# Next expert's down weights issued from ScalarE's queue, in a mixture-of-experts block on one Trainium2 core

## The reference

```python
# 4 groups of 8 experts, each expert 2048 -> 512 -> 2048; top group, then top 2 experts of it
eid = g_sel[:, None] * EXPERTS_PER_GROUP + top_i
gate = g_gate * softmax(top_v)
def expert_block(args):
    xb, e = args
    return (silu(xb @ w_gate[e]) * (xb @ w_up[e])) @ w_down[e]
ys = lax.map(expert_block, (xs, blk_expert))
out = segment_sum(ys * slot_gate[:, None], slot_tok)      # added to x
```

## Time and profile before

| | |
|---|---|
| median of 3 runs | 1783.31 us (1782.98 to 1784.92) |
| the profiled execution | 1783.29 us |
| its span in the profile | 1781.1 us |
| TensorE busy in the span | 1599.1 us (90%) |
| VectorE, ScalarE, GpSimd busy | 651.0, 345.0, 156.9 us |
| bytes moved by DMA | 484.42 MB, mean 272 GB/s |

### The profile page before, as it was taken

One profiled execution on the slowest core, in us unless ns is written; L12 is line 12 of the kernel. 1 busy time (PEld: TensorE's weight loads), 2 busy tenths in 40 slices (PEclk: granted clock), 3 DMA queues, 4 the chain that ended last, 5 costly groups with the idle time before them and its releaser, 6 DMA issues.

```text
span 1781.1 us, 19395 instructions
## 1 busy us (share of the span) xinstructions
PE 1599.1 (90%) x7339; PEld 909.5 (51%) x7339; DVE 651.0 (37%) x856; ACT 345.0 (19%) x612; POOL 156.9 (9%) x223
## 2 busy tenths in 40 slices
PE   7979999989999989939988988898898899889987
PEld 6567788868888445623343333333333334333333
DVE  1376676562223223351331332232132323323234
ACT  3122243452222133301101100100110010101001
POOL 0183024331000000010000000000000000000000
PEclk9989999999999999859999999999999999999999
DMA  7313321127222321319999999999999999999994
GB/s 285 95 32 87 94 72 48 48 71 243 95 95 98 162 79 64 148 37 408 421 421 421 422 421 422 422 421 422 422 422 422 421 422 422 421 421 420 421 421 192
DMA packets 114905, 484.42 MB, mean 272 GB/s; under 512 B 9410, under 2 KB 47404, under 8 KB 61868
## 3 DMA queue, kind: packets, MB, share of 16 engines
q1 hardware_dynamic: 110864, 470.84, 66.3%
q0 software_dynamic: 3264, 12.88, 1.9%
q10 hardware_dynamic: 732, 0.07, 0.0%
HBM read 484.81 MB, written 8.39 MB: 277 GB/s over the span
## 4 chain that ended last, share of the span: by engine, by line
PE 67%; DMA 21%; DVE 7%; issue 2%; ACT 2%; ACTq 0%; SPq 0%; POOL 0%; DVEq 0%; POOLq 0%
DMA weight_ring<-in_expert_w_up_dram 21%; PE ps L1813 17%; PE ps L1466 11%; PE ps L1571 10%; PE ps L1841 7%; PE ps L1680 3%; PE ps L1790 3%; PE ps L1624 3%; DVE residual L1351 2%; PE ps L1791 2%; PE ps L1426 2%; PE ps L1439 2%; PE ps L1706 1%; PE ps L1500 1%; PE ps L1535 1%
## 5 line engine op out<-in xcount | busy, mean ns | idle before, releaser
L1813 PE MATMUL ps<-weight_ring,transposed_acts 128*64 128x512 f32 x2048 | 469.0, 595 | 67.5 <-DMA weight_ring<-in_expert_w_up_dram 66.6
L1813 PEld LDWEIGHTS ps<-weight_ring,transposed_acts 128*64 128x64 f32 x2048 | 153.2, 137 | 377.3 <-issue 253.4
L1351 DVE TENSOR_TENSOR residual<-ps,residual 128x1024 f32<-128x1024 f32 x128 | 151.0, 1220 | 262.4 <-PE ps L1791 262.1
L1841 PE MATMUL ps<-weight_ring,transposed_acts 128*64 128x512 f32 x1024 | 226.8, 595 | 19.1 <-DVE transposed_acts L1358 19.1
L1369 DVE SCALAR_TENSOR_TENSOR y_low<-ps,proj_buffer,y_high 64x1024 fp32r<-64x1024 f32 x64 | 82.1, 1283 | 211.3 <-ACT y_high L851 210.2
L1841 PEld LDWEIGHTS ps<-weight_ring,transposed_acts 128*64 128x64 f32 x1024 | 71.8, 137 | 155.5 <-issue 152.6
L851 ACT ACTIVATE y_high<-ps,proj_buffer 64x1024 fp32r<-64x1024 f32 x64 | 71.0, 1109 | 306.3 <-PE ps L1841 305.4
L1790 PE MATMUL ps<-y_high,spread 128*128 128x512 f32 x256 | 113.8, 445 | 14.5 <-DVE residual L1351 10.4
L1466 PE MATMUL ps<-mix_high,w_in_high 128*128 128x512 f32 x288 | 117.7, 409 | 9.3 <-DVE w_in_low L960 9.3
L843 ACT ACTIVATE transposed_acts<-ps 128x512 f32<-128x512 f32 x32 | 19.1, 598 | 494.4 <-PE ps L1813 494.4
L1466 PE MATMUL ps<-mix_high,w_in_low 128*128 128x512 f32 x288 | 113.3, 393 | 0.0
(11 more groups left out here) (260 smaller groups left out, 1797.6 us busy)
## 6 DMA issues: line engine op xcount, KB each, us to landing
weight_ring<-in_expert_w_gate_dram SPq DMA_DIRECT2D x128, 1024.0 KB, 24.0
weight_ring<-in_expert_w_up_dram SPq DMA_DIRECT2D x128, 1024.0 KB, 25.9
weight_ring<-in_expert_w_down_dram SPq DMA_DIRECT2D x128, 1024.0 KB, 19.0
weight_ring<-in_w_in_dram SPq DMA_DIRECT2D x18, 1024.0 KB, 5.6
weight_ring<-in_w_out_dram SPq DMA_DIRECT2D x16, 1024.0 KB, 5.1
weight_ring<-in_xkv_w_dram SPq DMA_DIRECT2D x8, 1024.0 KB, 6.2
residual<-in_x_dram SPq DMA_DIRECT2D x8, 1024.0 KB, 19.1
weight_ring<-in_xq_w_dram SPq DMA_DIRECT2D x4, 1024.0 KB, 5.4
```

The costliest lines, as they stand in the source:

```text
L1351: v.tensor_tensor(part, ps[:, bank:bank + 2, :].rearrange("p b n -> p (b n)"), part, ALU.add).then_inc(sum_ready if last else part_added, 1)
L1813: ins = mm(ps[side * SLOTS:(side + 1) * SLOTS, 0, :], xsT[:, k, par * SLOTS:(par + 1) * SLOTS], w[:, kk, :], start=(k == 0), stop=(k == KD ...
L1841: ins = mm(ps[half, 4 + n // 2, :], act_t[:, f * SLOTS:(f + 1) * SLOTS], w[:, n * 512:(n + 1) * 512], start=(f == 0), stop=(f == KF - 1), ...
```

## The change

`load_expert` takes a count. In the loop over experts 1 to 31 SyncE issues 8 chunks, the gate and up ones, and ScalarE issues the four down chunks of the next expert, at the end of `block_act`, behind its two copies of the block's result. Their order on ScalarE comes from its own wait for `used`, which stands before the copies and is met when all four down chunks of the block are used. The last block of the 32 issues nothing, so the loop on ScalarE ends one pair earlier and that pair is written out. The blocks beyond the 32 are loaded by SyncE as before.

```diff
--- before.py
+++ after.py
@@ -431,20 +431,20 @@
                     sp.wait_ge(parts_done, 32)
                 sp.dma_start(slot(s), expert_chunk(0, j)).then_inc(landed[s], 16)
 
-            def load_expert(e, b):
-                for j in range(12):
+            def load_expert(e, b, count):
+                for j in range(count):
                     s = expert_slot(j)
                     sp.wait_ge(used, b * 12 + (UE - 12 + j + 1))
                     sp.dma_start(slot(s), expert_chunk(e, j)).then_inc(landed[s], 16)
 
             with sp.Fori(1, NE) as b:
-                load_expert(b, b)
+                load_expert(b, b, 8)
             sp.wait_ge(table_ready, 1)
             more = sp.value_load(meta[0:1, NOVER:NOVER + 1], min_val=0, max_val=NOVER)
             with sp.If(more > 0):
                 with sp.Fori(0, NOVER) as j:
                     e = sp.value_load(meta[0:1, ds(j, 1)], min_val=0, max_val=NE - 1)
-                    load_expert(e, j + NE)
+                    load_expert(e, j + NE, 12)
             for t in range(NT):
                 sp.wait_ge(sum_ready, 2 * t + 2)
                 sp.dma_start(out[0, t * P:(t + 1) * P, :], X[:, t, :]).then_inc(stored, 16)
@@ -837,7 +837,7 @@
             act.wait_ge(top_done, 1)
             a.activation(rq["et"], rq["dt"], ACT.Exp).then_inc(texp_done, 1)
 
-            def block_act(b, par):
+            def block_act(b, par, loads=False):
 
                 act.wait_ge(used, b * 12 + (UE + 8))
                 a.activation(gu, ps[:, 0, :], ACT.Copy).then_inc(gu_copied, 1)
@@ -850,14 +850,20 @@
                     rows = slice(side * SLOTS, (side + 1) * SLOTS)
                     a.activation(y_hi[par * SLOTS:(par + 1) * SLOTS, side:4:2, :], ps[rows, 4:6, :], ACT.Copy,
                                  scale=gate[rows, ds(b, 1)]).then_inc(y_act, 1)
+                if loads:
+                    for j in range(8, 12):
+                        s = expert_slot(j)
+                        act.dma_start(slot(s), expert_chunk(b + 1, j)).then_inc(landed[s], 16)
 
             act.wait_ge(table_ready, 1)
-            block_act(0, 0)
-            block_act(1, 1)
-            with act.Fori(1, NE // 2) as it:
+            block_act(0, 0, True)
+            block_act(1, 1, True)
+            with act.Fori(1, NE // 2 - 1) as it:
                 b = it * 2
-                block_act(b, 0)
-                block_act(b + 1, 1)
+                block_act(b, 0, True)
+                block_act(b + 1, 1, True)
+            block_act(NE - 2, 0, True)
+            block_act(NE - 1, 1)
             more = act.value_load(meta[0:1, NOVER:NOVER + 1], min_val=0, max_val=NOVER)
             with act.If(more > 0):
                 with act.Fori(NE // 2, NBLK // 2) as it:
```

## The result

The changed kernel takes 1818.99 us (1816.48 to 1820.44, 4 runs), the one before 1784.12 us: ratio 1.0193, 95% interval 1.0176 to 1.0211. It is 34.9 us slower; 8 us slower was forecast. The profiled execution took 1816.48 us, its span is 1814.3.

What follows compares the result with a forecast made beforehand. DMA bytes were taken to bound the expert loop. Order 7.0 us, holes 1, ScalarE 0 and start 0 summed to 8 us on 1783.3: 1791.3 us, likeliest case 1787 to 1796, outer range 1782.5 to 1825.

Steps and rivals of the forecast that it cites:

- The bound: Expert loop: DMA bytes at 421 to 422 GB/s set the pace; TensorE has 6 us a pair in hand.
- ScalarE's cost 0: End of each block: four issues, 2.1 us, fit into ScalarE's idle time, so they add 0 us.
- issue 0.4 us after the end of down: End of each block: ScalarE issues down loads 0.4 us after the last down matmul, bounds 0.3 and 2.4.
- Turns: DMA engines in the loop: the two queues are served equally, one 1 MB chunk of each in turn.
- N = 2.8: Even blocks: 2.8 down chunks land ahead of the last up chunk; bounds 1 to 4.
- Paid once, 7.0 us: Whole loop: down chunks landing early cost 7.0 us once, at the end, not per pair; bounds 2.5 to 10.
- Holes: DMA traffic at the end of even blocks: 0.3 us dry a pair, 0 to 4.5 over 15 pairs, taken as 1.
- U: Even block: the moment its last up chunk has landed; down of that block was put 20.6 us later.
- the wait would gather at the last step: Even blocks' gate/up: expected sign, TensorE's wait gathers at the last one or two steps, 3 us and more.
- Rival 1: DMA traffic runs dry each pair or expert: moderate 1806 to 1821 us, far end 1919; chance 0.26.
- Rival 2: Loop's two queues behave as one, or few down chunks land early: cost 0 to 3.5 us, 1783 to 1787; chance 0.16.
- Rival 3: Loop's DMA: a second queue raises the rate to 426 GB/s, giving 1772 or 1779 us; chance 0.10.

Runs made afterwards that it cites:

- e1: Changed kernel plus 24 filler matmuls on TensorE ahead of the last gate/up step of each even block: 2011.05 us, ratio 1.1274.
- e2: Kernel before the change plus the same 24 filler matmuls per even block, as a control: 2008.15 us, ratio 1.1254.
- e5: Changed kernel plus six filler matmuls ahead of the last gate/up step of each even block: 1795.36 us, ratio 1.0065.
- e11: Changed kernel with ScalarE issuing each down chunk as its slot is freed, plus six filler matmuls in even blocks: 1795.56 us, ratio 1.0058.
- e6: Kernel before the change plus six filler matmuls ahead of the last gate/up step of each even block, as a control: 1786.68 us, ratio 1.0010.
- e7: Changed kernel, but ScalarE issues each down chunk as its slot is freed, ahead of its two copies: 1792.85 us, ratio 1.0069.
- e9: Kernel before the change, one queue, but SP issues the four down chunks only after the block's last down matmul: 1785.23 us, ratio 1.0007.
- e4: Changed kernel, but ScalarE issues only odd experts' down chunks, at the end of even blocks; SP issues the rest: 1787.51 us, ratio 1.0020.
- e10: Kernel before, split in order of use: SP issues gate and down chunks 8, 10, ScalarE up and down chunks 9, 11, as slots are freed: 1784.64 us, ratio 0.9998.

## Why the prediction was wrong, step by step

- *The bound.* Right: e1 and e2 show it from the other side, where TensorE is the bound the change costs 3 us.
- *ScalarE's cost 0, and issue 0.4 us after the end of down.* Right: 0.5 us in the pair above.
- *Turns, and N = 2.8.* The mechanism was right, the size a little high for the pair shown: two down chunks landed ahead of the up chunk that ended the wait at 1246.67, at 1239.8 and 1244.7. The turns were equal there: down chunks landed at 1239.8, 1244.7 and 1249.8, gate and up chunks at 1241.6, 1246.6 and 1251.6. The Trainium skill, page "DMA: Bandwidth & Descriptors", section "Queues, rings and completion order", has each DMA engine go round robin between its queue rows; by these rows, the trace agrees.
- *Paid once, 7.0 us.* About right: 8.7 us in e5 and 8.9 in e11 over their control e6, 8.2 in e7 over the kernel before. In e11 nearly all of it is there by the second pair. In e5 only 3.9 us are; its other 4.6 us, 0.3 a pair, look like the small holes of the prediction (its window has 416 GB/s for 421), but the single holes were not measured.
- *Holes: 0.3 us a pair, "I take 1" in all.* This is the step that failed. It set U + 23.2 against 22.9 us of work, with TensorE's 20.6 us from U to the end of down copied from the kernel before. But in the kernel before the four waits of an even block are up to 1.6 us each and the clock stays at 1.00. I had written that the wait would gather at the last step, and did not ask what that does to the clock. The granted clock fell to 0.50, the step took up to 2.98 us more, and in the pair above, with the margin at nil, it became a hole of 2.7 us. Over the loop: 29.2 us of stretched steps, 21.3 us of delay from the second pair to the last, 23.6 us won back by fillers in their place, 26 us by an issue that does not hang on them.
- *Rival 1* named the place, the point from which it decides and, in its moderate form (1 to 2 us a pair, 1806 to 1821), the time, but with another cause, unequal turns; its sign, slices under 415 GB/s, came. It had a chance of 0.26. That the measured time lies inside the outer range, up to 1825, is owed to this rival and not to the sum. *Rival 2* did not come. *Rival 3* neither: 421 GB/s with two full queues.

The sum as the runs have it: 8 to 11 us for the order with its small holes, 24 to 26 for low clock and late issue together, which makes about 35. Two us of the profiled execution's lump at the start are a third thing, below.

## What to carry to other kernels

A queue of DMAs is an order. Before loads are moved to another queue, count what will land ahead of the chunk that is waited for, and how much work the DMA engines have left when the moved loads are released. Where many short waits are gathered into one long one, read the granted clock behind it: the work after the wait can get longer, and everything that is released by its end gets later. If an issue hangs on that end and the margin is nil, the loss is paid each time round; two queues filled in the order of use cost nothing.

## What the runs showed of the hardware that was not expected

- A few us of filler matmuls on TensorE made a DMA-bound kernel faster, 1819.0 to 1795.4 us, by keeping the clock at 1.00.
- TensorE's clock at the start of the loop differs between runs, whatever the kernel. In the window 797 to 805 after the change it was 0.68 and before 1.00:

```profile
797.00:805.00 8.00, 7.62 (x26) 2.40 (x28) 0.33 (x1) 0.00 (x0) 1.02 (x1) 0.68 0.25 69
```

```profile
797.00:805.00 8.00, 7.25 (x34) 2.50 (x36) 0.70 (x2) 0.00 (x0) 1.10 (x2) 1.00 0.51 159
```

  The first block's gate/up took 16.30 us for 13.95, and its copy came 2.0 us late. e9, whose TensorE code is that of the kernel before, had it too (0.62, 16.43 us) at 1785.23 us, e4 and e10 did not. So some 2 us of the profiled execution's 33 may be this; what decides it is open.
- A wait of 3 us and more does not always leave the clock low. In e4 the last step behind a wait of 3.06 us took 6.53 us (at 1384.66), and behind one of 3.02 us 3.65 us (at 1446.75); what decides between them is open. After the change all 14 such waits, 3.71 to 3.91 us, were followed by a slow step.
- A matmul of 128 x 128 weights on 512 columns in float32 took 0.87 us and left two records, so a filler is best measured alone first.
